# A two-block transformer on one core: a kept operand moved by 32 bytes, a first output projection that also norms and transposes, and expert weights fetched in thirds

## The reference, cut to what matters

```python
def first_block(x, ...):
    x = x + concat([y_rwkv, y_attn]) @ w_out      # first output projection
    return rmsnorm(x, final_g)

def second_block(x, ...):
    for l in range(2):
        h = rmsnorm(x, mix_norm[l])
        proj = h @ w_in[l]
        ...
        x = x + concat([a, r]) @ w_out[l]
        h = rmsnorm(x, ffn_norm[l])
        if l == 0:
            x = x + (silu(h @ w_gate) * (h @ w_up)) @ w_down
        else:
            x = x + moe(h, router, expert_gate, expert_up, expert_down)
    return rmsnorm(x, final_norm)
```

## Time and profile before

| | us |
|---|---|
| median of three runs | 5468.99 |
| the profiled execution's own time | 5473.01 |
| its span, first to last instruction | 5469.4 |
| last matmul of the first output projection to first of proj0 | 1096.17 to 1137.27 |
| proj0, first matmul to last | 1137.3 to 1343.2 |
| dense, first matmul with next_xT_high to last with next_xT_low | 1854.4 to 2267.7 |
| proj1, first matmul to last | 2527.3 to 2738.5 |
| experts, first matmul of the products to last | 3283.9 to 5398.3 |

### The profile page before, as it was taken

One profiled execution on the slowest core, in us unless ns is written; L12 is line 12 of the kernel. 1 busy time (PEld: TensorE's weight loads), 2 busy tenths in 40 slices (PEclk: granted clock), 3 DMA queues, 4 the chain that ended last, 5 costly groups with the idle time before them and its releaser, 6 DMA issues. The chain is left out here.

```text
span 5469.4 us, 92178 instructions
## 1 busy us (share of the span) xinstructions
PE 5092.8 (93%) x35964; PEld 4373.2 (80%) x35965; DVE 2685.9 (49%) x4387; ACT 2122.9 (39%) x3341; POOL 380.1 (7%) x613
## 2 busy tenths in 40 slices
PE   7996989979999999999989979999999999999994
PEld 5674977767777788887867768999999999999994
DVE  2597545431844655432165434444445555555444
ACT  2353236332444333332244423333334444444432
POOL 0111100000500100000032001000000000000001
PEclk8996999989999999999999989999999999999997
DMA  2110000221001222452100525444444555555545
GB/s 82 39 69 19 0 22 17 89 89 39 4 20 66 104 74 89 137 164 73 35 16 26 163 115 176 156 164 157 167 161 180 193 191 192 194 201 184 186 153 193
DMA packets 110462, 601.38 MB, mean 110 GB/s; under 512 B 13376, under 2 KB 17360, under 8 KB 80720
## 3 DMA queue, kind: packets, MB, share of 16 engines
q1 hardware_dynamic: 94208, 546.42, 28.4%
q0 software_dynamic: 12368, 38.97, 1.9%
q10 hardware_dynamic: 3712, 13.63, 0.6%
HBM read 529.35 MB, written 69.63 MB: 110 GB/s over the span
## 5 line engine op out<-in xcount | busy, mean ns | idle before, releaser
L3547 DVE TENSOR_TENSOR experts_low<-experts_raw,experts_high 128x1024 fp32r<-128x1024 f32 x678 | 810.5, 1223 | 955.5 <-ACT experts_high L3474 955.5
L3390 PE MATMUL ps<-experts_xs_high,experts_high 128*128 128x256 f32 (+1 forms) x3584 | 1031.2, 288 | 21.8 <-issue 13.4
L3390 PE MATMUL ps<-experts_xs_low,experts_high 128*128 128x256 f32 (+1 forms) x3584 | 1029.6, 287 | 0.0
L3390 PE MATMUL ps<-experts_xs_high,experts_low 128*128 128x256 f32 (+1 forms) x3584 | 1029.4, 287 | 0.0
L3474 ACT ACTIVATE experts_high<-experts_raw 128x1024 fp32r<-128x1024 f32 x678 | 687.8, 1049 | 44.3 <-DMA experts_raw<-experts 44.2
L3390 PEld LDWEIGHTS ps<-experts_xs_high,experts_high 128*128 128x128 f32 x3584 | 673.9, 188 | 33.3 <-issue 24.8
L3390 PEld LDWEIGHTS ps<-experts_xs_low,experts_high 128*128 128x128 f32 x3584 | 674.3, 188 | 8.3
L3390 PEld LDWEIGHTS ps<-experts_xs_high,experts_low 128*128 128x128 f32 x3584 | 674.2, 188 | 0.0
L3382 PE MATMUL ps<-experts_high,experts_hid_high 128*128 128x512 f32 x1120 | 438.4, 391 | 0.0
L3382 PE MATMUL ps<-experts_low,experts_hid_high 128*128 128x512 f32 x1120 | 437.2, 390 | 0.0
L3500 ACT ACTIVATE experts_silu<-ps 128x288 f32<-128x288 f32 (+1 forms) x224 | 88.8, 397 | 757.9 <-PE ps L3390 757.8
(11 more groups left out here) (603 smaller groups left out, 9234.1 us busy)
## 6 DMA issues: line engine op xcount, KB each, us to landing
experts_raw<-experts SPq DMA_DIRECT2D x226, 1536.0 KB, 6.4
dense_raw<-dense SPq DMA_DIRECT2D x56, 512.0 KB, 3.9
mixT<-w_in SPq DMA_DIRECT2D x36, 512.0 KB, 3.5
y_slot<-mla_blank SPq DMA_DIRECT2D x15, 1152.0 KB, 19.6
mixT<-dense SPq DMA_DIRECT2D x32, 512.0 KB, 3.8
out_proj_raw<-w_out SPq DMA_DIRECT2D x48, 256.0 KB, 2.8
proj_keys_raw<-w_in SPq DMA_DIRECT2D x20, 512.0 KB, 3.4
dense_raw<-hidden SPq DMA_DIRECT2D x32, 256.0 KB, 4.0
```

The lines of the kernel that those rows point to most:

```text
L3390: last = nc.tensor.matmul(ps[:, m, 0:width], w[:, u, m, c], x[:, k, 0:width], start=(k == 0 and i == 0), stop=(k == KD - 1 and i == 2))
L3547: nc.vector.tensor_tensor(low[:, v, t, :], raw[:, v % NR, t, :], high[:, v, t, :].bitcast(F32), ALU.subtract).then_inc(split, 1)
```

## The change

Three edits.

1. Before the kept operand is allocated, a tensor of 32 bytes (`right_edge`) is put at the right edge. `next_xT_high` then begins at 196,544 and `next_xT_low` at 163,776, multiples of 64.
2. The first output projection becomes `product_norms_and_turn`. It norms each row block twice, transposes it, and writes high and low parts over its own operand `first_xT_high` and `first_xT_low` (also at 196,544 and 163,776, behind a 32-byte `first_right_edge`); `proj0` and `inputs0` read them there, and the stage `mix_norm0` is gone. A block's transposes stand two blocks behind its product on PE. The first two blocks of `w_in0` are loaded after the store of block 4. To make room, `big` loses two of its five parts to `mixT`, which keeps the same addresses; the renaming of `big` to `front` and `big` in the RWKV stages moves no data.
3. An expert's chunk comes in three DMAs of 512 KB, each after the split of the same third two chunks before, and ACT waits for each third by itself.

```diff
+def product_norms_and_turn(core, name, operand, spare, weights, source, gain_row, normed, next_gain_row, xT, moves):
@@ product_norms_and_turn, SP @@
+            for b in range(NT):
+                sp.wait_ge(scaled, b + 1)
+                sp.dma_start(normed[b * P:(b + 1) * P, :], x[:, b, :]).then_inc(stored[min(b, 2)], 16)
+                if b == 4:
+                    sp.wait_ge(stored[0], 16)
+                    sp.wait_ge(stored[1], 16)
+                    sp.wait_ge(next_scaled, 2)
+                    for to, origin in moves:
+                        sp.dma_start(to, origin).then_inc(beside, 16)
@@ product_norms_and_turn, PE @@
+            def turn(b):
+                pe.wait_ge(next_scaled, b + 1)
+                if b == 0:
+                    pe.wait_ge(added, NT)
+                if b >= 2:
+                    pe.wait_ge(lowered, b - 1)
+                for k in range(KD):
+                    last = nc.tensor.transpose(turn_bank(b)[:, k, :], ready[b % 4][:, k * P:(k + 1) * P], core.c("eye"))
+                last.then_inc(turned, 1)
...
+                for k in range(K):
+                    if b == 0:
+                        pe.wait_ge(split, K + k + 1)
+                    last = three(BANKS[b % 3], k, b)
+                last.then_inc(product, 1)
+                if b >= 2:
+                    turn(b - 2)
+            turn(NT - 2)
+            turn(NT - 1)
@@ product_norms_and_turn, ACT @@
+            for b in range(NT):
+                square(1, b)
+                if b >= 1:
+                    take_next_root(b - 1)
+                take_root(b)
+                if b >= 2:
+                    place(b - 2)
+                square_next(b)
+            take_next_root(NT - 1)
+            place(NT - 2)
+            place(NT - 1)
@@ product_norms_and_turn, DVE @@
+            for b in range(NT):
+                add(1, b)
+                if b >= 1:
+                    average_next(b - 1)
+                average(b)
+                if b >= 1:
+                    invert_next(b - 1)
+                invert(b)
+                if b >= 1:
+                    scale_next(b - 1)
+                scale(b)
+                if b >= 2:
+                    lower(b - 2)
+            average_next(NT - 1)
+            invert_next(NT - 1)
+            scale_next(NT - 1)
+            lower(NT - 2)
+            lower(NT - 1)
...
@@ expert_passes @@
-            def fetch(e, f, v):
-                row = e * NC + f
-                src = weights[bass.ds(row, 1)].rearrange("a p n -> p (a n)")
-                sp.dma_start(raw[:, v, :, :].rearrange("p a n -> p (a n)"), src).then_inc(loaded[v], 16)
+            def fetch(e, f, v, t):
+                src = weights[bass.ds(e * NC + f, 1)].rearrange("a p n -> p (a n)")[:, t * D:(t + 1) * D]
+                sp.dma_start(raw[:, v, t, :], src).then_inc(loaded[v][t], 16)
...
-                        sp.wait_ge(split, 3 * (j * NC + f + 1) + SPLIT0)
                         over = isinstance(f, int) and f + AHEAD >= NC
-                        fetch(e_next if over else e, f + AHEAD - NC if over else f + AHEAD, u % NR)
+                        for t in range(3):
+                            sp.wait_ge(split, 3 * (j * NC + f) + t + 1 + SPLIT0)
+                            fetch(e_next if over else e, f + AHEAD - NC if over else f + AHEAD, u % NR, t)
...
-                if t == 0:
-                    act.wait_ge(loaded[v % NR], n_loads)
+                act.wait_ge(loaded[v % NR][t], n_loads)
...
@@ build @@
-        first_block(core, dump)
+            xT = first_block(core, mixT, turned, dump)
...
-                mix_layer(core, 0, table, mixT, dram["x_block"], dram["x_mixed0"], dump)
+                mix_layer(core, 0, table, mixT, dram["x_block"], dram["x_mixed0"], dump, xT, turned)
+                turned.enter_context(nc.sbuf_tensor("right_edge", [P, 8], F32, side="right"))
                 xT = tuple(turned.enter_context(nc.sbuf_tensor(f"next_xT_{part}", [P, KD, T], F32R, side="right")) for part in ("high", "low"))
...
@@ first_block @@
-        product_and_norm(core, "out_proj", flat[:, 0:8, :], d["w_out"], d["x"], d["final_g"], d["x_block"])
+        turned.enter_context(nc.sbuf_tensor("first_right_edge", [P, 8], F32, side="right"))
+        xT = tuple(turned.enter_context(nc.sbuf_tensor(f"first_xT_{part}", [P, KD, T], F32R, side="right")) for part in ("high", "low"))
+        product_norms_and_turn(core, "out_proj", mixT[:, :, :], flat, d["w_out"], d["x"], d["final_g"], d["x_block"], d["mix_row0"], xT,
+                               [(mixT[:, u, :], d["w_in0"][u]) for u in range(2)])
```

More of the change, by code:

```diff
@@ L427, in projections, with rwkv_operands @@
     st.end()
-def rwkv_operands(core, big, small, decay_end, bonus, rate, cum):
+def rwkv_operands(core, front, big, small, decay_end, bonus, rate, cum):
     nc, d = core.nc, core.dram
@@ L982, in rwkv_chunks, with rwkv_output_and_queries @@
     st.end()
-def rwkv_output_and_queries(core, big, gate, bonus, out, queries, latent_T, latent, w_uv, q_abs):
+def rwkv_output_and_queries(core, front, big, gate, bonus, out, queries, latent_T, latent, w_uv, q_abs):
     nc, d = core.nc, core.dram
     st = Stage(core, "rwkv_out")
-    dev, sq, Y = big[:, 2], big[:, 3], big[:, 1]
+    dev, sq, Y = big[:, 0], big[:, 1], front[:, 1]
     stat = st.sb("stat", [P, 3, 8 * NT])
@@ L3257, in expert_passes @@
     y_tail = st.sb("y_tail", [TAIL, D])
-    loaded = [st.sem(f"loaded{i}") for i in range(NR)]
+    loaded = [[st.sem(f"{part}_loaded{i}") for part in ("gate", "up", "down")] for i in range(NR)]
     (indexed, gathered, turned, x_high, x_low, rounded, split, gate_made, up_made, silu_done, hid_made, hid_rounded, hid_split, down,
@@ L3303, in _ @@
                     sp.wait_ge(gathered, 48)
-                fetch(first, f, f)
+                for t in range(3):
+                    fetch(first, f, f, t)
             with sp.Fori(0, NPASS, 1) as j:
@@ L3675, in build @@
                 mix_layer(core, 1, table, mixT, dram["x_ffn"], dram["x_mixed1"], dump, xT, turned)
-            expert_ffn(core, dram["x_mixed1"], dram["out"])
+        expert_ffn(core, dram["x_mixed1"], dram["out"])
 def expert_ffn(core, source, out):
@@ L3744, in as_rows, with first_block @@
     return x.rearrange("p a n -> p (a n)").rearrange("p (b n) -> p b n", b=NT)
-def first_block(core, dump):
+def first_block(core, mixT, turned, dump):
     nc, d = core.nc, core.dram
-    with nc.sbuf_tensor("big", [P, 5, 4, T], F32) as big:
+    front = mixT[:, :, :].rearrange("p (a j) n -> p a j n", a=2)
+    with nc.sbuf_tensor("big", [P, 3, 4, T], F32) as big:
         flat = big[:, :, :, :].rearrange("p a j n -> p (a j) n")
         with nc.sbuf_tensor("masks", [P, offset(NT) - offset(TOPK // P)], F32) as masks, nc.sbuf_tensor("small", [P, T], F32) as small:
-            down, queries, relu = flat[:, 0:4, :], flat[:, 8:10, :], flat[:, 10:12, :]
+            down, queries, relu = mixT[:, 0:4, :], flat[:, 0:2, :], flat[:, 2:4, :]
             with nc.sbuf_tensor("index_weight", [P, NT, IDX_HEADS], F32) as weight, ExitStack() as s2:
                 xT = split_tensors(core, s2, "xT", [P, KD, T])
-                norm_transpose(core, "norm_in", as_rows(flat[:, 0:8, :]), xT, "norm_row", d["x"], eye=d["constants"][:, 0:P],
+                norm_transpose(core, "norm_in", as_rows(mixT[:, :, :]), xT, "norm_row", d["x"], eye=d["constants"][:, 0:P],
                                moves=[(core.vec[:, :], d["vectors"]), (core.cst[:, P:NCST], d["constants"][:, P:NCST])])
@@ L3765, in first_block @@
                 projections_and_keys(core, "proj_keys", d["w_in"], 5, xT,
-                                     [(4, ACT.Copy, lambda n: flat[:, n + 4, :], None), (8, ACT.Copy, lambda n: flat[:, n + 12, :], None),
+                                     [(4, ACT.Copy, lambda n: mixT[:, n + 4, :], None), (8, ACT.Copy, lambda n: flat[:, n + 4, :], None),
                                       (4, ACT.Silu, None, d["spill_gate"]), (4, ACT.Silu, None, d["spill_gate2"])],
@@ L3770, in first_block @@
             with nc.sbuf_tensor("space", [P, 8, T], F32) as space, nc.sbuf_tensor("bonus", [P, 4, T], F32) as bonus,                     nc.sbuf_tensor("decay_end", [P, 4, NCH], F32) as decay_end:
[L3771 to L3772 removed]
+                rwkv_operands(core, front, big, small, decay_end, bonus, space[:, 0:4], space[:, 4:8])
+                rwkv_chunks(core, front, big, decay_end, [(space[:, 0:4, :], d["spill_gate"])])
                 latent_T = small
[L3774 to L3775 removed]
+                q_abs = lambda n: space[:, 4 + n, :] if n < 4 else front[:, 1, n - 4, :]
+                o_lat = flat[:, 0:8, :]
                 with nc.sbuf_tensor("latent_rows", [P, NT, P], F32) as latent, nc.sbuf_tensor("value_up", [P, 8, P], F32) as w_uv:
[L3777 removed]
+                    rwkv_output_and_queries(core, front, big, space[:, 0:4], bonus, mixT[:, 0:4, :], big[:, 2], latent_T[:, :], latent[:, :, :],
```

172 lines of the change are left out of this document (155 added, 17 removed).

## The result

The changed kernel takes 5432.04 us (median of four runs, 5428.24 to 5435.81) against 5468.93 for the kernel before: a ratio of 0.9931, 95% interval 0.9919 to 0.9944, or 36.9 us less. Measured again beside the last experiments it took 5430.10 (five runs) against 5469.24, ratio 0.9927 (0.9913 to 0.9940). The profiled execution of the changed kernel took 5434.67 with a span of 5430.6, 38.3 less than that of the kernel before.

What follows compares the result with a forecast made beforehand. PE was taken to bound the dense stage and the experts, and to stand still before proj0 and at the experts' start. Gains of 12.9 + 20.2 + 7.0 = 40.1 us take the median from 5468.99 to 5428.9, range 5421 to 5444.

Steps and rivals of the forecast that it cites:

- The 32 bytes: proj1, inputs1, dense: matmuls with next_xT lose 7 or 5 ns each once shifted; 12.9 us together, bounds 10.6 to 14.8.
- The doubt that the experts' down products raised: Both their operands lie 32 past yet run at 387/389, so the cost may need one operand off and one on.
- The projection: First output projection to proj0: PE's standstill of 40.7 falls to 15.0, less 5.5 for turns; 20.2 us, bounds 16.0 to 21.6.
- The gap: From the first output projection's last matmul to proj0's first: 40.7 us before, 15.0 forecast after the change.
- The six turns in the loop: First output projection: five of the six stand before the last product, each 1.1 us on full PE, 5.5 us more.
- the 0.7 us of margin: First output projection's loop: DVE's 5.9 us a block against PE's 6.6; if lost, PE waits about 1 us a late block.
- The thirds: Experts' start: PE resumes 6 to 8 us earlier at chunk 1's up product; 7.0 us taken, bounds 0 to 9.8.
- the wait that was described: Experts' start: PE stands 8.4 us before chunk 1's up product, behind chunk 2's splits and its 12.1 us transfer.
- the shift restores nothing: Rival: the right-edge region itself is slow, so proj0 and inputs0 pay 6.6 us; gain 20.6, 5448.4 us; chance 0.08.
- the thirds bring nothing: Rival: the experts' start stall stays because other traffic, not size, stretched the wait; 5435.9 us; chance 0.10.
- thirds land one after the other: Rival: in the experts a chunk would take 11.7 us, PE waiting 3.4 each, 381 us more, 5817; chance 0.03.

Runs made afterwards that it cites:

- the shift alone: Only the 32 bytes at the right edge added to the kernel before: 5454.41 us, ratio 0.9974 to the kernel before.
- the second address run: Changed kernel with next_xT and its partner operands in dense and proj1 put 32 past a multiple of 64, inputs1's weights unmoved: 5429.54 us, ratio 0.9921.
- the late scatters: POOL's scatters wait for the third chunk's weights to be split: on the changed kernel 5427.85 and 5426.42 us, on the kernel before 5463.13.
- the experts on 64: Changed kernel with the experts' token list allocated ahead of their weights, so weights and hidden products begin at multiples of 64: 5439.99 us, ratio 0.9949.

## Why the prediction was right

It said 5428.9, within 5421 to 5444; 5432.0 and 5430.1 were measured. Each of the three gains came where it was forecast, the third in a size that varies from run to run. That the whole lies so near is in part luck: in the two profiles, whose times differ by 38.3, a loss of some 4.5 us and a gain of some 3.2 at TensorE's lower clock level, which no term holds, largely cancel; both are told below.

**The 32 bytes: 12.9 said, 13.8 measured** by the shift alone (interval of the ratio: 8 to 20 us). Dense's line with `next_xT_high` gave 402.1 − 395.3 = 6.8 from first to last start, for 6.3. From start to start dense's products with the low part gained as much as those with the high one, 6.5 ns on average (233.3 to 226.8), where 5 and 7 had been taken: 2112 at 6.5 are 13.7. Inputs1's line hardly moved, 45.9 to 45.8 us, though its steps at the upper clock level went from 235 to 227 ns: more of its first matmuls, 15 steps against 10, ran slowly. Proj1's line with the shift alone runs 205.0 us, 5.3 less than before, as said. In the changed kernel's profile it is 8.5 less, because a stretch at the lower clock level is missing there. Windows of the same products, before and in the changed kernel (the third number from the end is the granted clock):

```profile
2644.00:2651.00 7.00, 7.00 (x24) 5.85 (x24) 1.37 (x3) 1.06 (x1) 0.00 (x0) 0.59 0.21 68
```

```profile
2620.00:2627.00 7.00, 7.00 (x33) 5.79 (x32) 0.62 (x3) 0.00 (x0) 0.00 (x0) 1.00 0.24 77
```

The kernel with the late scatters has the stretch in its first profile and not in its second (212.3 and 208.8 us from proj1's first matmul to inputs1's first), so one program shows both, and the 3.2 us are not counted to the change.

The doubt that the experts' down products raised, that it takes one operand off and one on, is what the second address run shows. The page "SBUF — State Buffer" of the Trainium skill, section "Specifications (TRN2)", with its lines of 16 bytes, sees no difference between a start at a multiple of 64 and one 32 past it; the trace shows 7 ns, and the measurement decides.

**The projection: 20.2 said, 20.0 in its place, 17.7 over the whole (interval 11.5 to 24.6).** From out_proj's first matmul to proj0's first it took 1137.3 − 1007.5 = 129.8 us and takes 1119.75 − 1009.94 = 109.8; in the other profiles with the new function and `first_xT` aligned the gain is 20.1 to 21.0. The gap is 15.4 for 15.0. The six turns in the loop lengthen the products by 5.3 for 5.5, and no wait of PE's appeared: the 0.7 us of margin held. What the sum did not hold is far ahead of it, in the norms of the latent rows. Windows from 100 to 106 us, of the kernel before, of the changed one, and of the kernel with `first_xT` 32 past:

```profile
100.00:106.00 6.00, 4.55 (x28) 3.22 (x27) 1.23 (x1) 4.64 (x12) 0.00 (x0) 1.00 0.01 4
```

```profile
100.00:106.00 6.00, 4.42 (x12) 2.15 (x11) 0.00 (x0) 3.58 (x11) 0.00 (x0) 0.56 0.02 4
```

```profile
100.00:106.00 6.00, 5.18 (x30) 3.91 (x30) 1.22 (x1) 4.05 (x5) 0.00 (x0) 0.93 0.01 4
```

At the same work PE had 28 matmuls done by 106 us at a granted clock of 1.00 before, and 12 at 0.56 after; the next stage begins at 148.1 in place of 143.5. So about 4.5 us were lost there, in all six profiles of four kernels: the changed kernel (twice), it with late scatters (twice), the new projection alone and the experts on 64. Four other kernels with the same new projection (the third row is one of them) and all four with the old one did not lose it. In two kernels that were profiled twice it fell out alike both times, but two pairs do not show that it hangs on the program. Among the eight with the new projection the tensors of that stage lie at the same addresses, and in both groups PE had rested 1.81 us before the stage's transposes and 1.37 to 1.58 before its first product. What goes with it in all fourteen profiles is the clock some 57 us earlier. Windows from 43 to 47 us, in the first products, before and in the changed kernel:

```profile
43.00:47.00 4.00, 4.00 (x14) 3.13 (x14) 0.00 (x0) 0.00 (x0) 0.00 (x0) 0.71 0.31 111
```

```profile
43.00:47.00 4.00, 4.00 (x12) 3.08 (x11) 0.00 (x0) 0.00 (x0) 0.00 (x0) 0.61 0.42 144
```

In the six profiles with the loss the mean granted clock there is 0.61 to 0.68, in the other eight 0.71 to 0.95: where the clock rose later, it later fell earlier. These first products are the same in every kernel here, with their operands at the same addresses. What sets the difference stays open, and that the loss belongs to the change is not shown.

**The thirds: 7.0 said, 5.1 measured** by the thirds alone (interval of the ratio: 0 to 10 us), within the bounds of 0 to 9.8. PE's first gate matmul and its first matmul of chunk 1's up product, in the profile of that run:

```profile
3278.48 0.37 PE L3391 MATMUL ps<-experts_xs_high,experts_high 128*128 128x288 f32 x1 [1.71 <-DVE experts_xs_low L3542]
...
3289.86 0.37 PE L3391 MATMUL ps<-experts_xs_high,experts_high 128*128 128x288 f32 x1 [1.54 <-issue]
```

The second starts 11.4 us after the first, where it was 18.2 (3283.87 to 3302.11): 6.9 earlier, by the wait that was described. In the changed kernel's first profile it is 15.3, only 2.9 earlier, and the term that failed there is the thirds' time beside the scatters: chunk 2's second third took 8.8 us, where 3.9 to 7.4 had been taken, and chunk 1's own last third 12, which ACT rounds before it may turn to the first silu. In its second profile it is 11.4 again. So the gain varies from run to run: 14.7 to 18.5 us from gate to down, 4 to 8 less than before. In the passes nothing was won or lost, as said: from first down to last 2091.8 us after and 2091.3 before.

**The rivals.** That the shift restores nothing is refuted by its run alone. That the thirds bring nothing is not what the first chunks show, though the interval of their own run touches it; its ground, that other traffic stretched the wait, is what the late scatters bear out. That thirds land one after the other is refuted: 36 of them land in 100 us of the passes with a median of 4.2 us, 12 chunks as before. The rule of the Trainium skill's page "DMA: Bandwidth & Descriptors", section "Rules for kernel authors", to make a DMA of at least 1 MiB for most bandwidth, would have spoken against the thirds; here 512 KB transfers kept up, since the matmuls of a chunk need 8.3 us and its three thirds did not arrive later than that. The prediction's estimate by the formula of that page of the Trainium skill, which the page gives for transfers that GpSimd issues, was 3.2 us for a third and 5.6 for a chunk; SP's transfers took 4.2 and 6.3 in the median.

## What to carry to other kernels

Before pricing an alignment, compare the two operands of a matmul with each other, not each with a round number: at 512 columns a pair that lay differently by 32 bytes cost 7 ns here and a pair that lay alike cost nothing, both on a multiple of 64 or both 32 past one; in the experts' narrower products aligning brought no gain. A stall at a stage's start has several waits queued behind one another; a price for removing the first is an upper bound until the second is found. A fused stage keeps what was counted in its own place, but the whole should be read from the first instruction on: in some profiles 4.5 us were lost a millisecond earlier, and in some 3.2 were gained later on, and no run ties either to the change.

## What was not expected of the hardware

The step from one matmul to the next is 227 ns at 512 columns for aligned pairs and for pairs both 32 past, 233 for mixed ones; at 256 columns the mixed pair is the fastest of the three, 117 against 118 (both off) and 120 (both on). Beside small scatters the weight transfers fell from about 400 GB/s to 8 to 115 for 4.5 us, though the DMA view counts 0.00 MB for the scatters' queue. The granted clock fell to the lower level at the start of one short stage in six profiles and some 5 us later in eight, with the same instructions there; in the six it had also risen later, 57 us before.
